# Packing four heads of 32 sample tokens into one tile of 128 rows, in both mixers of a hybrid decoder trunk

## The chip, the cores and the metric

The kernel is one launch on one core of a Trainium2 chip. The metric is the device time of that launch in microseconds (us). The core's engines each work through a queue of their own, in order: TensorE (PE in the profile, PEld for its weight loads), VectorE (DVE), ScalarE (ACT), GpSimd (POOL) and SyncE (SP). They meet at semaphores. TensorE writes only the eight banks of PSUM.

## What is computed

One step of a two-layer decoder for two groups of tokens that share the weights: a prompt of 1024 tokens, and 8 sample sequences of 4 new tokens each (32 tokens) that carry recurrent states. Width 1024, 4 heads.

- Layer 0: a gated DeltaNet mixer (with a spatial gating branch beside it), then a squared-ReLU MLP of width 4096.
- Layer 1: an mLSTM mixer, then the same kind of MLP.

For the sample tokens the gated delta rule comes to this, per sequence `b` and head `h`, on 4 tokens:

```
sol = triangular_solve(I + A, [v * beta, kb * exp(gc)])      # A: masked k k^T, decayed
v_new = u_c - wk_c @ S                  # S: state, 128 x 128
o = qd_c @ S + qk_c @ v_new
S = S * gl_c + kd_c^T @ v_new
```

and the mLSTM to this, with C of 128 x 256 and a vector n of 128 for each `b`, `h`:

```
num = w_inter * (q @ C) + s @ v
den = w_inter * (q @ n) + sum(s)
h = num / max(|den|, exp(-m_t))
C = keep * C + (wk * k)^T @ v
n = keep * n + sum(wk * k)
```

Everything that is not per sequence (scores, decays, solve) is done for all 32 tokens of a head at once under a mask of 4x4 blocks; the products with the states are done for each of the 32 pairs (b, h).

## The kernel before

**Dense work.** The projections and MLPs are a list of units. A unit loads 1024 columns of weights into `wst`, ScalarE rounds them into `whi`, VectorE computes the rest into `wlo` (`lo(u)`, L1665), and TensorE makes three products for each 128x128 block (high·high, low·high, high·low), every record 512 columns wide for prompt tokens 0 to 511 (group 0) or 2 x 272 for the rest with the samples (group 1). A unit is cut into four pieces (`("d", u, p)`); for group 0 a piece is 6 records. `whi` and `wlo` have two buffers. `lo(u + 1)` stands in VectorE's program behind piece 1 of unit u. VectorE also adds the results of the second MLP matrix into the accumulator (L1740) and computes `h1lo` (L1681).

**Mixer work** is spread between those pieces. `Plan.mix` takes the rows of dense pieces and a list `side` of mixer steps, and puts `len(side)/len(rows)` steps behind each row; `("rest",)` is an empty step that only holds a place. All engines run through this one order, so a step's place fixes where it stands on each queue. The samples' delta rule runs in units 102 to 117 (MLP of layer 0, group 0), beside and behind the prompt's tiles 4 to 7; the samples' mLSTM in units 277 to 294 (MLP of layer 1, group 0).

**The samples' steps of the delta rule** (tile `t == TILES`, n = 32): `dec`, `kk`, `kT`, `vT`, `l0`, `la`, `lb`, `zw`, `oT` in `gdn(t, step, q)` do each thing head by head, as four products or transposes of 32 rows. `gdn_sample("vn", j)` makes v_new of heads 2j, 2j+1: for each head one product of the inverse with the right side, then 8 products (one per sequence) of `NWM` (128x32, the columns of the other sequences zeroed) with the state `SS[:, h % 2, b]`, all summed in PSUM. `"o"` does the same with `QDM` for the output. `"u"` makes four state updates at a time: stationary `KM` (32x128), moving `VN` (32x128); VectorE multiplies the old state by its decay and adds (L2052). `SS` holds two heads; POOL stores a head when it is done and loads head h + 2 into its place.

**The samples' steps of the mLSTM**: `mA`, `mB`, `mC`, `mF` in `ml(t, step)`, and in `ml_sample`: `"num"` (per head: 8 products of `QDM` (128x32) with C and n, 257 columns, and one of the scores with v) and `"dc"` (four updates of C: stationary 32x128, moving 32x257; VectorE folds them in, L2209). `CS` holds two heads of C; POOL stores a head (L2636) and loads the head after next (L2591). `rowmask`-products on VectorE (L2039, L2196) zero the keys of the other sequences, 32x512 at a time.

**Records.** A float32 product (`mm`, L605) shows in the trace as two MATMUL records and two LDWEIGHTS records, a transpose as one of each.

Of the kernel before, what the change touches and what calls it, by code (L numbers as in the profile page):

```python
# [5 lines left out]
F32 = mybir.dt.float32  # L6
F32R = mybir.dt.float32r
ALU = mybir.AluOpType
# [25 lines left out]
NL = LEVELS - LB  # L34
FG = 8
# [40 lines left out]
class Plan:  # L76
# [92 lines left out]
    @staticmethod  # L169
    def gdn_sample():  # L170
        t = TILES
        out = [("gx", t), ("gx2", t)] + [("g", t, s, 0) for s in ("act", "gv", "sum", "dec", "kk", "kT", "vT", "l0")]
        out += [("g", t, "la", 1), ("g", t, "lb", 1), ("g", t, "zw", 0), ("gs", "km", 0), ("rest",)]
        for j in range(2):

            out += [("rest",)] * (2 * j) + [("gs", "vn", j), ("gs", "o", j), ("rest",)]
            for h in (2 * j, 2 * j + 1):
                out += [("gs", "u", 2 * h), ("gs", "u", 2 * h + 1), ("rest",)]
            out.append(("rest",))
        out += [("gs", "end", 0), ("rest",), ("rest",), ("rest",), ("g", t, "oT", 0)]  # L180
        return out

    @staticmethod
    def ml(tiles):
        out = []
        for t in tiles:
# [9 lines left out]
            else:  # L196
                out += [("m", t, s) for s in ("mA", "mB", "mC")]
                out.append(("ms", "km", 0, 0))
                for h in range(H):
                    out += [("ms", "num", h, 0), ("ms", "dc", h, 0), ("rest",), ("ms", "dc", h, 1), ("rest",)]  # L200
                out += [("ms", "end", 0, 0), ("rest",), ("rest",), ("m", t, "mF")]
# [129 lines left out]
def build(nc, x_prompt, x_sample, state_gdn, state_gdn_conv, state_mlstm_c, state_mlstm_n, state_mlstm_m,  # L331
# [4 lines left out]
    with ctx:  # L336
# [28 lines left out]
        maskposS = sb("maskposS", [NS, NS])  # L365
        masknegTS = sb("masknegTS", [NS, NS])
# [3 lines left out]
        lmask = sb("lmask", [P, LEVELS, P])  # L370
        lmask0T = sb("lmask0T", [P, P])
        rowmask = sb("rowmask", [NS, NB])
# [62 lines left out]
        def inv_at(t, q, p):  # L435

            return t * (3 + 2 * NL) + (2 * (q - LB) + p + 4 if t < TILES else 2 * q + p + 1)

        def t2_at(t, q, p):

            return t * 2 * NL + 2 * (q - LB if t < TILES else q) + p + 1

        def x_at(t, q, p):

            return t * 2 * NL + 2 * (q - LB if t < TILES else q - 1) + p + 1

        def gdn_map(t):
            n = P if t < TILES else NS
            keys = ["X", "QH", "SQ", "RB", "DT", "QD", "XX", "KB", "KD", "RU", "VB"]
            shapes = [(NCH, n), (8, n), (8, n), (8, n), (H, n), (H, n), (2, 4, n), (H, n)] + [(H, P)] * 3  # L450
            if n == NS:
                keys += ["RW", "NW", "NWM", "QDM", "KM", "SS"]
                shapes += [(H, P), (H, n), (H, NB, NS), (H, NB, NS), (2, 4, P), (2, NB, P)]
# [3 lines left out]
            m["ON"], m["VN"] = m["VB"] if n == P else m["RW"], m["RU"]  # L457
            m["Xi"] = lambda h: m["XX"][0:n, 0, h, :]
# [14 lines left out]
        def ml_map(t):  # L473
# [3 lines left out]
            else:  # L477
                keys = ["X", "WTm", "E", "ST", "KW", "HN", "QDM", "KM", "CS", "NT", "NN", "NROW", "NPR", "BC"]
                shapes = [(NCH, NS)] + [(H, NS)] * 3 + [(H, P), (H, DV + 1), (H, NB, NS), (2, 4, P),
                                                        (2, NB, DV + 1), (NB, H), (NB, H), (P,), (P,), (2, H, NS)]  # L480
# [122 lines left out]
        def _(pe):  # L603
# [186 lines left out]

            def gdn(t, step, q):
                m = gdn_map(t)
                g, c, n = tok(t)
                X, QH = m["X"], m["QH"]
                lv = LEVELS if t < TILES else LEVELS_S
# [33 lines left out]
                elif step == "vT":  # L829
                    w("vsr")  # L830
                    if n == P:
                        w("ke")
                        w("state")
                        for h in range(H):
                            pe.matmul(M4(3)[:, h, :], X[:, 8 + h, :], ident[:, :], is_transpose=True,
                                      start=True, stop=False)
                            last = mm(M4(3)[:, h, :], m["KB"][:, h, :], St[:, h, :], start=False, stop=True)
                    else:
                        for h in range(H):
# [1899 lines left out]
```

## Time and profile before

| | |
|---|---|
| median of 3 runs | 2650.51 us (2650.06 to 2651.29) |
| span of the profiled execution | 2647.3 us |
| TensorE busy | 2584.7 us (98%) |
| VectorE, ScalarE, POOL busy | 1380.3, 1128.1, 244.2 us |
| samples' delta rule | about 815 to 915 us |
| samples' mLSTM | about 1952 to 2087 us |

How to read it: a time such as 845.02 is us from the start of the span; the next number is the duration. A record's duration is its way through a pipeline and overlaps the next one, so what a group of records costs is read from its start to the start of the dense record behind it. `x16` is 16 records merged into one row. `128*32` ahead of the operand's shape is the stationary operand, rows by columns; the last shape is the moving operand.

### The profile page before, as it was taken

The numbers are of one execution on the slowest core, as the hardware profiler recorded it, in microseconds if no ns is written. First come the engines' busy times: TensorE is split into PE (matmuls) and PEld (weight loads), VectorE is DVE, ScalarE is ACT, GpSimd is POOL, SyncE is SP. The second block draws the span as 40 slices with busy tenths as digits, with TensorE's granted clock in tenths as the row PEclk, the third lists the DMA queues.
The fourth block names the chain that finished last, engine by engine and source line by source line (L and its number), as shares of the span: only waits on it lengthen the run. The fifth ranks groups of instructions, "written<-read, shape, count | busy, mean of one in ns | idle before, by whom it ended". The sixth has DMA issues, their size and how long they took to land.

```text
span 2647.3 us, 39319 instructions
## 1 busy us (share of the span) xinstructions
PE 2584.7 (98%) x16324; PEld 2307.5 (87%) x16324; DVE 1380.3 (52%) x2201; ACT 1128.1 (43%) x1914; POOL 244.2 (9%) x396
## 2 busy tenths in 40 slices
PE   8998999999999999999999999999999999999998
PEld 7778888788887798899999989998877888999998
DVE  4746765656564565434444465535544456454344
ACT  6654446455444245333333345433332345333324
POOL 4121111100001001100000001110000000000000
PEclk9999999999999999999999999999999999999999
DMA  6553335533333455533333245554444343333322
GB/s 205 157 156 106 104 113 135 154 101 85 106 95 92 120 144 168 170 120 112 105 95 111 83 131 151 165 150 123 120 120 146 102 121 122 87 111 106 96 88 82
DMA packets 368722, 321.47 MB, mean 121 GB/s; under 512 B 11930, under 2 KB 339668, under 8 KB 368545
## 3 DMA queue, kind: packets, MB, share of 16 engines
q1 hardware_dynamic: 336224, 207.91, 27.2%
q0 software_dynamic: 32320, 111.05, 13.8%
q8 instruction: 130, 2.13, 0.3%
q14 instruction: 48, 0.39, 0.0%
HBM read 261.33 MB, written 57.58 MB: 120 GB/s over the span
## 4 chain that ended last, share of the span: by engine, by line
PE 85%; DVE 6%; ACT 5%; DMA 2%; issue 2%; SPq 0%; POOL 0%; DVEq 0%; ACTq 0%; POOLq 0%
PE dense L605 75%; PE mixer L605 8%; ACT arena L1148 2%; DVE wlo L1665 1%; ACT whi L1148 1%; DMA wst<-in_w_in_even_dram 1%; DVE arena L1890 0%; DVE hf L1806 0%; ACT relu L1148 0%; ACT L1148 0%; DVE hlo L1802 0%; ACT L1153 0%; DMA arena<-xrow 0%; DVE arena L1892 0%; PE mixer L995 0%
## 5 line engine op out<-in xcount | busy, mean ns | idle before, releaser
L605 PE MATMUL dense<-hhi,whi 128*128 128x272 f32 (+1 forms) x3072 | 847.9, 330 | 22.0 <-DVE wlo L1665 15.3
L605 PE MATMUL dense<-hhi,wlo 128*128 128x272 f32 (+1 forms) x3072 | 824.9, 323 | 0.0
L605 PE MATMUL dense<-hlo,whi 128*128 128x272 f32 (+1 forms) x3072 | 824.2, 323 | 0.0
L1665 DVE TENSOR_TENSOR wlo<-wst,whi 128x1024 fp32r<-128x1024 f32 x384 | 471.7, 1228 | 233.2 <-ACT whi L1148 232.3
L605 PEld LDWEIGHTS dense<-hhi,whi 128*128 128x128 f32 x3072 | 515.8, 189 | 78.8 <-DVE wlo L1665 21.1
L1148 ACT ACTIVATE whi<-wst 128x1024 fp32r<-128x1024 f32 x384 | 403.8, 1052 | 423.9 <-PE dense L605 410.5
L605 PEld LDWEIGHTS dense<-hhi,wlo 128*128 128x128 f32 x3072 | 514.1, 189 | 41.7
L605 PEld LDWEIGHTS dense<-hlo,whi 128*128 128x128 f32 x3072 | 516.4, 189 | 37.4 <-issue 0.7
L605 PE MATMUL dense<-h1hi,whi 128*128 128x272 f32 (+1 forms) x1536 | 422.5, 329 | 9.3 <-DVE wlo L1665 5.0
L605 PE MATMUL dense<-h1hi,wlo 128*128 128x272 f32 (+1 forms) x1536 | 414.0, 324 | 0.0
L605 PE MATMUL dense<-h1lo,whi 128*128 128x272 f32 (+1 forms) x1536 | 412.1, 322 | 0.0
L605 PEld LDWEIGHTS dense<-h1hi,whi 128*128 128x128 f32 x1536 | 256.8, 188 | 38.3 <-DVE wlo L1665 8.6
L1681 DVE TENSOR_TENSOR h1lo<-relu,h1hi 128x544 fp32r<-128x544 f32 (+1 forms) x128 | 91.6, 715 | 369.3 <-ACT relu L1148 369.2
L605 PEld LDWEIGHTS dense<-h1hi,wlo 128*128 128x128 f32 x1536 | 257.2, 188 | 21.5
L605 PEld LDWEIGHTS dense<-h1lo,whi 128*128 128x128 f32 x1536 | 257.2, 188 | 21.0 <-issue 0.5
L1148 ACT ACTIVATE relu<-dense 128x512 f32<-128x512 f32 (+2 forms) x132 | 80.6, 611 | 383.8 <-PE dense L605 383.6
L605 PE MATMUL mixer<-arena 128*128 128x128 f32 (+11 forms) x1552 | 231.0, 293 | 11.1 <-DVE arena L1972 8.6
L605 PEld LDWEIGHTS mixer<-arena 128*128 128x128 f32 (+5 forms) x1552 | 193.9, 173 | 50.3 <-issue 21.2
L1740 DVE TENSOR_TENSOR accA<-dense,accA 128x512 f32<-128x512 f32 (+1 forms) x168 | 116.1, 697 | 103.4 <-PE dense L605 103.1
L1756 DVE TENSOR_TENSOR ssum<-ssum,sq 128x512 f32<-128x512 f32 (+1 forms) x98 | 69.2, 707 | 125.7 <-ACT sq L1148 125.6
L1148 ACT ACTIVATE ffh<-dense 128x512 f32<-128x512 f32 (+5 forms) x124 | 62.2, 525 | 167.7 <-PE dense L605 155.7
L1148 ACT ACTIVATE arena<-mixer 128x128 f32<-128x128 f32 (+9 forms) x175 | 63.4, 376 | 101.5 <-PE mixer L605 59.4
(352 smaller groups left out, 1813.6 us busy)
## 6 DMA issues: line engine op xcount, KB each, us to landing
wst<-in_w_ff_dram SPq DMA_DIRECT2D x256, 512.0 KB, 4.0
wst<-in_w_in_even_dram SPq DMA_DIRECT2D x48, 512.0 KB, 4.1
wst<-in_w_in_odd_dram SPq DMA_DIRECT2D x48, 512.0 KB, 4.0
proj<-ffh POOLq DMA_DIRECT2D x48, 272.0 KB, 2.6
proj<-ffh POOLq DMA_DIRECT2D x48, 256.0 KB, 2.3
arena<-proj POOLq DMA_DIRECT2D x16, 512.0 KB, 4.9
wst<-in_w_out_even_dram SPq DMA_DIRECT2D x16, 512.0 KB, 4.1
arena<-proj POOLq DMA_DIRECT2D x8, 1024.0 KB, 8.2
```

Source lines behind the costliest of these rows:

```text
L605: return pe.matmul(out, lhsT, rhs, start=start, stop=stop)
L1148: return act.activation(out, in_, func, **how)
L1665: TT(wlo[:, u % 2, :], wst[:, u % 2, :], whi[:, u % 2, :].bitcast(F32), ALU.subtract)\
L1681: TT(h1lo[:, k, 0:n], r, h1hi[:, k, 0:n].bitcast(F32), ALU.subtract)\
L1740: TT(v, out_of(key, g), v, ALU.add).then_inc(S("dve_evac"), 1)
L1756: ins = TT(ssum[:, 0:n], ssum[:, 0:n], sq2[:, c % 2, 0:n], ALU.add)
```

## The change

Head h's 32 tokens take rows 32h to 32h+31 of one tile of 128 rows.

- Steps that did four heads one after another do one 128x128 product or transpose (`gdn_rows`, `ml_rows`), under masks that are zero between heads. Gates per row come from a product with `spread4` and a masked sum (`own_head`).
- Products with the states stay 32 pairs, but each goes to the band of its head. For v_new, o and num the band is 32 output partitions (the output is `MB[rows_at(h), ...]`); for the updates it is 32 rows of both operands (`KM[rows_at(h), ...]`), and the four heads write four PSUM banks. The loops run over sequences outside and heads inside, so that neighbouring products are in different bands.
- n leaves the 257th column of C: it has a step of its own (`"n"`, two products), and C's products are 256 wide.
- All four heads of the delta rule's state are loaded at once; nothing of it is loaded again. Of C, four sequences (all heads) are in `CS`; sequences 4, 5 and 6, 7 are loaded after 0, 1 and 2, 3 have been stored.
- `vn` and `o` become `vo` (v_new and the state's part of o) and a short `o`; the updates `u` come in two steps of 16 behind `oT`. `num` has two steps and `dc` four steps of 8 updates. The side list of the delta rule is 11 steps shorter and that of the mLSTM 2, which spreads the remaining steps, those of prompt tiles 4 to 7 too, a little wider over the same dense rows.
- The masks at the start are 128 wide instead of 32, and `lmask` has 5 levels instead of 7.

```diff
@@ Plan
-        out += [("g", t, "la", 1), ("g", t, "lb", 1), ("g", t, "zw", 0), ("gs", "km", 0), ("rest",)]
-        for j in range(2):
-
-            out += [("rest",)] * (2 * j) + [("gs", "vn", j), ("gs", "o", j), ("rest",)]
-            for h in (2 * j, 2 * j + 1):
-                out += [("gs", "u", 2 * h), ("gs", "u", 2 * h + 1), ("rest",)]
-            out.append(("rest",))
-        out += [("gs", "end", 0), ("rest",), ("rest",), ("rest",), ("g", t, "oT", 0)]
+        out += [("g", t, "la", 1), ("g", t, "lb", 1), ("g", t, "zw", 0), ("rest",), ("rest",), ("gs", "vo", 0)]
+        out += [("rest",), ("gs", "o", 0), ("rest",), ("gs", "end", 0), ("rest",), ("g", t, "oT", 0), ("rest",)]
+        out += [("gs", "u", 0), ("rest",), ("rest",), ("rest",), ("gs", "u", 1), ("rest",), ("rest",), ("rest",)]
...
+                out += [("m", t, s) for s in ("mA", "mB", "mC")] + [("ms", "n", 0), ("rest",)]
+                for r in range(2):
+                    out += [("ms", "num", r), ("rest",)]
+                    for half in (2 * r, 2 * r + 1):
+                        out += [("ms", "dc", half), ("rest",), ("rest",)]
+                    out += [("rest",)] * (1 - r)
+                out += [("ms", "end", 0), ("rest",), ("rest",), ("m", t, "mF")]
@@ tensor, delta rule
+                elif step == "la":
+                    w("inv", inv_at(t, q - 1, 0))
+                    s(mm(bank(0), rows_of(m["A"]), m["XiT"]), "t2")
...
+                if step == "vo":
...
+                    mm(MB[:, 1, 0:P], m["XiT"], m["RU"], start=True, stop=False)
+                    for b in range(NB):
+                        for h in range(H):
+                            last = mm(MB[rows_at(h), 1, 0:P], m["NWM"][:, h, b, :], m["SS"][:, h, b, :],
                                       start=False, stop=b == NB - 1)
...
+                    for b in range(NB):
+                        for h in range(H):
+                            mm(MB[rows_at(h), 2, 0:P], m["QDM"][:, h, b, :], m["SS"][:, h, b, :],
+                               start=b == 0, stop=False)
...
                     for k in range(4):
-                        last = mm(M4(3 * q)[:, k, :], m["KM"][0:n, q, k, :], m["VN"][0:n, h, :])
+                        for h in range(H):
+                            last = mm(MB[:, h, k * P:(k + 1) * P], m["KM"][rows_at(h), 4 * r + k, :],
+                                      m["VN"][rows_at(h), :])
@@ tensor, mLSTM
+                    for b in range(4 * r, 4 * r + 4):
+                        pe.wait_ge(S(f"s_in{b // 2 % 2}"), 32 * (r + 2))
+                        for h in range(H):
+                            last = mm(MB[rows_at(h), 0, 0:DV], m["QDM"][:, h, b, :], m["CS"][:, b % 4, h, :],
+                                      start=r == 1 and b == 4, stop=b % 4 == 3)
...
+                    for b in (2 * r, 2 * r + 1):
+                        for h in range(H):
+                            last = mm(MB[:, h, b % 2 * DV:(b % 2 + 1) * DV], m["KM"][rows_at(h), b, :],
+                                      V1[rows_at(h), 0, 0:DV])
@@ gpsimd
+                if name == "dc":
+                    pool.wait_ge(S("ms_upd"), r + 1)
+                    for b in (2 * r, 2 * r + 1):
+                        dma(c_s[0, b].rearrange("h k v -> k h v"), m["CS"][:, b % 4]).then_inc(S(f"s_out{r % 2}"), 16)
+                    if r < 2:
+                        pool.wait_ge(S(f"s_out{r}"), 64)
+                        for b in (2 * r, 2 * r + 1):
+                            cs_load(b + 4)
```

TensorE, the first state products of the delta rule. Before, v_new of heads 0 and 1 (18 products) and, six dense records later, their output:

```order
L605 MATMUL mixer<-arena 32x128 x18
L605 MATMUL dense<-h1hi_49,whi 128x512
L605 MATMUL dense<-h1lo_50,whi 128x512
L605 MATMUL dense<-h1hi_49,wlo 128x512
L605 MATMUL dense<-h1hi_49,whi 128x512
L605 MATMUL dense<-h1lo_50,whi 128x512
L605 MATMUL dense<-h1hi_49,wlo 128x512
L605 MATMUL mixer<-arena 32x128 x18
```

Now, all heads' v_new and state output in a row (the first row is the product with the inverse):

```order
L624 MATMUL dense<-h1hi_49,wlo 128x512
L624 MATMUL mixer<-arena 128x128
L624 MATMUL mixer<-arena 32x128 x64
L624 MATMUL dense<-hhi0,whi 128x512
```

Four groups of 18 have become one of 65 and, one unit further on, a single product.

VectorE, the state updates of the delta rule (`gls` holds the decays, `wlo` is `lo(u)`). Before, the first two groups of four:

```order
L2052 SCALAR_TENSOR_TENSOR arena<-arena,gls,mixer 128x128 x4
L2039 TENSOR_TENSOR arena<-arena,rowmask 32x512
L1665 TENSOR_TENSOR wlo<-wst,whi 128x1024
L1740 TENSOR_TENSOR accA<-dense,accA 128x512
L2052 SCALAR_TENSOR_TENSOR arena<-arena,gls,mixer 128x128 x4
```

Now, the first of the two groups, in unit 115:

```order
L1794 TENSOR_TENSOR h1lo<-relu,h1hi 128x512
L2218 SCALAR_TENSOR_TENSOR arena<-arena,gls,mixer 128x128 x16
L1778 TENSOR_TENSOR wlo<-wst,whi 128x1024
L1794 TENSOR_TENSOR h1lo<-relu,h1hi 128x512
L1778 TENSOR_TENSOR wlo<-wst,whi 128x1024
```

Sixteen updates stand in a row now, directly ahead of `lo(116)`.

POOL, the state C of the mLSTM. Before:

```order
L2636 DMA out_dram<-arena 128x8x256
L2591 DMA arena<-in_state_mlstm_c_dram 128x8x256
L2636 DMA out_dram<-arena 128x8x256
L2591 DMA arena<-in_state_mlstm_c_dram 128x8x256
```

Now:

```order
L2811 DMA out_dram<-arena 128x4x256 x2
L2757 DMA arena<-in_state_mlstm_c_dram 128x4x256 x2
L2811 DMA out_dram<-arena 128x4x256 x2
L2757 DMA arena<-in_state_mlstm_c_dram 128x4x256 x2
```

A store or load of 1 MB has become two of half a megabyte; they are bound to sequences now, not to heads.

## Rows read from the trace of the kernel before

**Rows 1.** The page: span, busy time, share of the chain that ended last.
```profile
span 2647.3 us, 39319 instructions
PE 2584.7 (98%) x16324; PEld 2307.5 (87%) x16324; DVE 1380.3 (52%) x2201; ACT 1128.1 (43%) x1914; POOL 244.2 (9%) x396
PE 85%; DVE 6%; ACT 5%; DMA 2%; issue 2%; SPq 0%; POOL 0%; DVEq 0%; ACTq 0%; POOLq 0%
```
**Rows 2.** TensorE by stretches of the samples' stages; first all, then the mixer's bank alone.
```profile
815.00:915.00 100.00, 99.18 (x555) 77.80 (x554) 45.40 (x98) 34.52 (x71) 6.47 (x7) 1.00 0.35 102
1955.00:2090.00 135.00, 133.87 (x577) 97.40 (x577) 64.21 (x111) 38.22 (x65) 7.54 (x10) 1.00 0.44 134
...
815.00:915.00 100.00, 32.85 (x272) 1.00 0.35 102
1955.00:2090.00 135.00, 35.18 (x154) 1.00 0.44 134
```
**Rows 3.** Timeline of TensorE, delta rule: start, duration, engine, line, operation, shapes, records.
```profile
819.39 0.69 PE L605 MATMUL mixer<-arena 128*32 128x32 f32 x16
820.02 0.50 PE L605 MATMUL dense<-hhi,whi 128*128 128x512 f32 x1
820.35 0.39 PE L605 MATMUL dense<-hlo,whi 128*128 128x512 f32 x1
820.58 0.40 PE L605 MATMUL dense<-hhi,wlo 128*128 128x512 f32 x1
...
827.70 0.23 PE L848 MATMUL mixer<-ident,arena 32*32 32x32 f32 x2 [0.82 <-ACT arena L1148]
...
845.02 4.46 PE L605 MATMUL mixer<-arena 32*32 32x128 f32 x36
849.41 0.50 PE L605 MATMUL dense<-h1hi,whi 128*128 128x512 f32 x1
...
859.47 0.39 PE L605 MATMUL dense<-h1hi,wlo 128*128 128x512 f32 x1
859.79 1.15 PE L605 MATMUL mixer<-arena 32*128 32x128 f32 x8
860.87 0.50 PE L605 MATMUL dense<-h1hi,whi 128*128 128x512 f32 x1
```
**Rows 4.** The same for the weight loads (PEld).
```profile
836.07 1.86 PEld L605 LDWEIGHTS mixer<-arena 32*128 32x128 f32 x16 [0.35 <-issue]
...
845.02 0.13 PEld L605 LDWEIGHTS mixer<-arena 32*32 32x32 f32 x2 [0.36 <-issue]
845.35 1.67 PEld L605 LDWEIGHTS mixer<-arena 128*32 128x32 f32 x16 [0.20 <-issue]
847.22 0.13 PEld L605 LDWEIGHTS mixer<-arena 32*32 32x32 f32 x2 [0.20 <-issue]
```
**Rows 5.** Timeline of TensorE, full 128x128 transpose and product (prompt tile), and mLSTM.
```profile
747.19 0.27 PE L835 MATMUL mixer<-ident,arena 128*128 128x128 f32 x1
747.29 0.39 PE L605 MATMUL mixer<-arena 128*128 128x128 f32 x2
747.52 0.27 PE L835 MATMUL mixer<-ident,arena 128*128 128x128 f32 x1
...
1968.68 4.21 PE L605 MATMUL mixer<-arena 128*32 128x257 f32 x18
1972.83 0.50 PE L605 MATMUL dense<-h1hi,whi 128*128 128x512 f32 x1
...
1977.15 2.00 PE L605 MATMUL mixer<-arena 32*128 32x257 f32 x8
1979.07 0.50 PE L605 MATMUL dense<-hhi,whi 128*128 128x512 f32 x1
```
**Rows 6.** Timeline of VectorE around a group of state updates in each mixer.
```profile
901.51 1.12 DVE L2052 SCALAR_TENSOR_TENSOR arena<-arena,gls,mixer 128x128 f32<-128x128 f32 x4 [7.02 <-PE mixer L605]
902.55 0.67 DVE L2039 TENSOR_TENSOR arena<-arena,rowmask 32x512 f32<-32x512 f32 x1
...
1985.11 1.23 DVE L1665 TENSOR_TENSOR wlo<-wst,whi 128x1024 fp32r<-128x1024 f32 x1 [0.26 <-ACT whi L1148]
1986.85 1.78 DVE L2209 SCALAR_TENSOR_TENSOR arena<-arena,keepb,mixer 128x257 f32<-128x257 f32 x4 [0.52 <-PE mixer L605]
```
**Rows 7.** POOL's timeline and the DMA view (KB, us to landing): one state is exchanged.
```profile
1988.92 0.90 POOL L2636 DMA_DIRECT2D out_dram<-arena  x1 [38.47 <-DVE arena L2209]
1994.27 0.88 POOL L2591 DMA_DIRECT2D arena<-in_state_mlstm_c_dram  x1 [4.44 <-DMA out_dram<-arena]
...
arena<-in_state_mlstm_c_dram POOLq DMA_DIRECT2D x4, 1024.0 KB, 7.7
```

More of the change, by code:

```diff
@@ L34 @@
 NL = LEVELS - LB
+LMASK = {q: i for i, q in enumerate([*range(LEVELS_S), *range(LB, LEVELS)])}
 FG = 8
@@ L791, in gdn @@
             def gdn(t, step, q):
+                if t == TILES and step != "sum":
+                    gdn_rows(step, q)
+                    return
                 m = gdn_map(t)
@@ L1035, in ml_sample @@
[L1035 to L1044 removed]
+                        pe.wait_ge(S("ms_upd"), 2)
@@ L1904, in gdn @@
             def gdn(t, step, q):
+                if t == TILES and step != "sum":
+                    gdn_rows(step, q)
+                    return
                 m = gdn_map(t)
@@ new lines, in ml_sample @@
+                if step == "n":
+                    dve.wait_ge(S("ms_n"), 1)
+                    keep = keepb[:, :, 4:].rearrange("p h b -> p b h")
+                    link(TT(m["NN"], m["NT"], keep, ALU.mult))
+                    part = lambda a: MB[:, 3, a:a + NB * H].rearrange("p (b h) -> p b h", h=H)
+                    TT(m["NN"], m["NN"], part(192), ALU.add)
+                    link(TT(m["NT"], part(128), own[:, :, :], ALU.mult))
+                    dve.tensor_reduce(mcol[:, 3:4], m["NT"].rearrange("p b h -> p (b h)"),
+                                      mybir.AxisListType.X, ALU.add).then_inc(S("ms_nset"), 1)
+                elif step == "num" and r:
+                    dve.wait_ge(S("ms_num"), 2)
+                    TT(m["HN"][:, 0:DV], m["HN"][:, 0:DV], MB[:, 0, 0:DV], ALU.add).then_inc(S("ms_kept"), 1)
+                elif step == "dc":
+                    dve.wait_ge(S("ms_dc"), r + 1)
+                    for b in (2 * r, 2 * r + 1):
+                        for h in range(H):
+                            cs = m["CS"][:, b % 4, h, :]
+                            last = STT(cs, cs, keepb[:, h, 4 + b:5 + b], MB[:, h, b % 2 * DV:(b % 2 + 1) * DV],
+                                       ALU.mult, ALU.add)
+                    last.then_inc(S("ms_upd"), 1)
@@ L2623, in ml_x @@
                         .then_inc(S("m_xin"), 16)
-                    cs_load(0)
-                    cs_load(1)
+                    for b in range(4):
+                        cs_load(b)
             def ml(t, name):
```

661 lines of the change are left out of this document (380 added, 281 removed).

## The prediction

> **What bounds the kernel now.** I read the page first. TensorE is busy 98% of the span, and the chain that ended last lies 85% on it, while VectorE is busy 52% [rows 1]. Then the two stretches in which the samples' steps run: 99.18 of 100 us and 133.87 of 135 us of TensorE are busy, VectorE about half, and the granted clock is 1.00, the 2.4 GHz level [rows 2]. Records on the mixer's bank hold 32.85 and 35.18 us of these stretches [rows 2]. So in both stages TensorE's own queue is what ends last: work taken off it comes off the time, and work of other engines counts only where TensorE waits for it. The only wait of size on the samples' path is 0.82 us before the transposes of `l0` [rows 3].
>
> **Prices on TensorE** (from a group's start to the next dense record, which itself comes every 0.23 us [rows 3]):
>
> - Entering and leaving a group costs 0.19 us more than the records: 859.79 - 859.47 = 0.32 in, 820.35 - 820.02 = 0.33 out, each 0.23 otherwise, so 0.09 + 0.10 [rows 3].
> - State product of v_new or o (stationary 128x32, 128 columns): 16 records in 1.67 us, 0.104 a record, 0.21 a product [rows 4]. With 257 columns: 18 records in 4.15, 0.46 a product [rows 5].
> - Update (stationary 32x128): 128 columns 0.96 us of TensorE's pace for four (1.08 from start to start, 0.12 of it the edge), 0.24 a product; 257 columns 1.92 for four, 0.48 [rows 3, 5].
> - Full product 0.23 (747.52 - 747.29), full transpose 0.10 [rows 5].
> - Change of shape inside a group: 0.33 less two records of 0.104 is 0.12, up to the 0.20 that PEld shows as idle [rows 4].
>
> **The change part by part, if bands do not overlap.**
>
> State products of the delta rule: before, four groups of 4.39 us (849.41 - 845.02) and 0.19 each, 18.3 us [rows 3]. After, 64 products at 0.208 are 13.3, two full ones 0.46, edges 0.38, one change 0.16: 14.3. Gain 4.0, since eight small products and most shape changes go. Updates: 8 x (1.08 + 0.19) = 10.2 before; 32 x 0.24 + 2 x 0.3 = 8.3 after. Gain 1.9.
>
> Packed steps of the delta rule: before, `kk` 0.63 [rows 3], `zw` 1.89 (16 records paced by their weight loads, 1.86) [rows 4], six groups of four small transposes or products at about 0.36 and `l0` with its wait 1.2, some 5.9 us. After, `kk` two products 0.46, `kT`, `vT`, `l0`, `oT` one transpose each 0.4, `la` and `lb` 0.46, `zw` one full product and four of 32x128 weights 1.17, `dec` one product more 0.6: 3.1. Gain 2.8, the wait of 0.82 in it: `l0` now comes a unit behind `kk` with no wait on ScalarE's `ru`. Delta rule together 8.7.
>
> mLSTM: `num` 4 x (4.15 + 0.19) = 17.4; after, 33 products at 0.46 and 0.38 make 15.6: 1.8. `dc` 8 x (1.92 + 0.19) and a wait, 17.4; after, 32 x 0.48 + 4 x 0.19 = 16.2: 1.2 [rows 5]. Transposes of v and h go from 16 to 4 records, the scores from four products to one, two products of n and one of the gates are new: gain about 1.0. Together 4.0.
>
> So 12.7 us without any overlap.
>
> **Overlap between bands.** No row of before shows two products in different bands. The bounds come from neighbouring rows. At one end a band changes nothing and the gain above stands. At the other end all four bands run together and a product costs a quarter. I take the middle, for this reason: a product is two records that write the same rows of PSUM, so the second has to follow the first in its band, and if records start in program order, the next head's first record can only start with this head's second. Then two bands run at a time, and a product costs one record instead of two. Floors: a record with 32x128 weights doesn't go below 0.118 us however few its columns (`zw`: 1.89 us for 16 records with 32 columns, and the weight loads fill it) [rows 4]; one with 128x32 weights went at 0.039 (0.63 us for 16) [rows 3]. Hence:
>
> - v_new and o: 64 x 0.104 = 6.7 us gained.
> - num: 32 x 0.23 = 7.4.
> - dc: 32 x 0.24 = 7.7; half of 0.48 is 0.24, just at the floor of two weight loads, 0.236.
> - u: 0.24 is at the floor already, gain 0.
>
> Together 21.8.
>
> The Trainium skill (TensorE: Matmul & The Clock Gate, Part 3) gives 3.07 times the speed for four row bands and 2.38 for three column bands at 512 columns; as an estimate from it, the 51 us of banded products would shrink by some 32 us where I take 21.8. No row of before can show it. Its page TensorEngine Tiling (Key Properties) says that changing the tiling mode drains the array and changing only the tile does not; the 0.12 to 0.20 us above are shape changes, so they agree with the first half, and the second half is what is open here.
>
> **What is late next.** Two waits on TensorE are new.
>
> (1) The exchange of C. Before, from the last update (1986.85 + 1.78) to the landing of the reload (1994.27 + 7.7) took 13.3 us [rows 6, 7]; nobody waited, since the next use of that head lay two heads further on. Now stores and loads are two each, so about 15.1 us (two more issues of 0.9). `dc` 1 stands behind piece 2 of unit 284, `num` 1 behind piece 0 of unit 287: ten pieces of six records, 13.8 us. Counted from the start of `dc` 1 with overlap: TensorE 2.1, VectorE 8 x 0.445 = 3.6 [rows 6], exchange 15.1: landed at 20.9. TensorE asks for sequences 6 and 7 at 2.1 + 13.8 + 0.2 + 1.9 = 18.0. It waits 2.9 us, and in-order dense work waits behind it. Without overlap the same sum gives 22.7 against 21.6, 1.1 us.
>
> (2) Sixteen updates ahead of `lo(116)`. They take 16 x 0.26 = 4.2 us (902.55 - 901.51 is four) and `wlo` 1.23 more [rows 6], so it is ready 5.6 us after `u` 0 ends on TensorE. TensorE has three pieces of unit 115, 4.1 us, and two records, 0.5, before it needs it: wait 1.0. The second group stands behind piece 3 of its unit, and `lo` comes out level; 0.2. The four groups of eight (3.6 us) stand behind piece 2, with `lo` of their unit done already: 0.
>
> Costed at nothing: the key masks on VectorE (8 x 0.67 us per mixer become one pass of about 1.2, hidden under dense work at half load), the wider masks on POOL at the start and three reductions on VectorE there (POOL is busy 9%), the state loads of 2 MB some 40 us ahead of `vo`, the prompt's steps moved by up to four units (same distances or longer; I allow 2 us either way). If the cover of the key masks went, they would cost 1.2 us each.
>
> Sum: 12.7 + 21.8 - 2.9 - 1.2 = 30.4 us less. 2650.5 - 30.4 = 2620.1. The span of 2647.3 lies 3.2 below the median, and I take that as constant.
>
> **The rivals.**
>
> A. Bands don't overlap: 12.7 - 1.1 - 1.2 = 10.4 less, 2640. For it: no row shows an overlap, and records of one shape in the same place queue strictly at their column time. Against it: the bands share neither rows nor banks (updates) or neither columns nor output rows.
>
> B. All four bands run together, weight loads too: the banded 51.1 us (13.3 + 14.7 + 15.4 + 7.7) shrink to 12.8, the reload wait grows to about 4: 12.7 + 38.3 - 5 = 46 less, 2604. Against it: the floor of 0.118 us for 32x128 weights [rows 4] and the shared band of a product's two records. This is where the skill's speed-ups would lead, its estimate above ending near 2610.
>
> C. Slower: every change of band costs what a change of shape costs. There are 64 + 32 + 32 + 32 = 160 such products, each in another band than the one before. At 0.12 to 0.20 us that is 19 to 32 us, and the time 9 to 22 us above the median, 2666 at the 0.16 in between. It decides from 10.4 / 160 = 0.065 us per change. For it: rows 4 show the cost wherever the array is addressed in another way. Against it: in those rows the size of the stationary operand changed as well, here it stays.
>
> D. The bands overlap on one side only (columns, or rows): 30.4 less 7.7, or less 14.1; 2628 to 2634.
>
> **How the numbers follow.** Forecast (two at a time) 0.48, A 0.20, B 0.10, C 0.10, D 0.12. The likeliest gives 2620.1. The range leaves out C and most of B: 2610 to 2643, which takes in A with the allowance of 2 us. A measurement of this kernel can tell about 0.2%, 5.3 us. All but C, and the part of A in which the two waits are larger than I count, come out faster by more: faster 0.85, same 0.05, slower 0.10.
>
> **What would show it.** In the profile of the changed kernel: 64 products of `vo` in about 7 us (forecast), 13.3 (A), 3.5 (B), over 20 (C). Sixteen products of `num` in 3.7 us or 7.4. Eight updates of `dc` in 1.9 us or 3.8. `u` at 3.9 us for sixteen; well below that, the floor of the weight loads is wrong for bands. A wait of TensorE for the load of C of 1 to 3 us near the second `num`, and one of about 1 us for `wlo` behind the first `u`. TensorE's busy time on the mixer's bank falls from 68 us to about 34. The forecast is wrong if the trace shows other rates, or if the waits on TensorE in the delta rule's tiles 4 to 7 grow by more than 2 us.

## The result, and the profile after

The changed kernel took 2609.98 us (median of 4 runs, 2607.28 to 2610.32) against 2650.3 us (2650.06 to 2651.29) on the same chip: a ratio of 0.9843, 95% interval 0.983 to 0.9857. It is 40.3 us faster. The forecast was 30.4 less, 2620, and the range began at 2610: the direction was right, the size was not, and the time lies just under the range.

The page of the changed kernel, its span, engines and the chain that ended last. It answers to [rows 1].

```profile
span 2605.6 us, 39107 instructions
PE 2540.0 (97%) x16251; PEld 2280.9 (88%) x16251; DVE 1372.1 (53%) x2173; ACT 1122.9 (43%) x1885; POOL 251.0 (10%) x406
...
PE 84%; DVE 7%; ACT 5%; DMA 2%; issue 2%; POOL 0%; DVEq 0%; ACTq 0%; POOLq 0%
```

TensorE is still the bound: 44.7 us less busy time, 41.7 us less span. On the mixer's bank its records hold 27.1 us of the two stretches of the samples' steps (813 to 913 and 1952 to 2087 us), where the forecast had about 34 and the kernel before 68. To see where the time went, I cut both traces at the layers' norm sums, which TensorE makes in both kernels. The window view gives, for TensorE in the two stages that hold the samples' steps (delta rule, then mLSTM), the length, busy us, records, granted clock, DMA share and GB/s. Before:

```profile
471.92:944.93 473.01, 464.14 (x2410) 1.00 0.37 105
1676.51:2151.41 474.90, 470.83 (x2573) 1.00 0.44 128
```

After:

```profile
471.11:928.36 457.25, 444.84 (x2358) 0.99 0.38 109
1660.47:2109.46 448.99, 446.33 (x2551) 1.00 0.46 135
```

The delta-rule stage is 15.8 us shorter and the mLSTM stage 25.9, together the whole change; the stretch between them takes 731.6 and 732.1 us. In the first stage TensorE's idle time grew from 8.9 to 12.4 us, in the second it fell from 4.1 to 2.7.

TensorE's timeline after, the groups that the prediction priced, each with the dense record behind it. In order: v_new with the state's part of o (64 banded products and a full one), an update `u` of 16 products, one `dc` of 8 updates, and the second `num`, cut in two by its wait.

```profile
868.66 4.01 PE L624 MATMUL mixer<-arena 128*128 128x128 f32 x130
872.60 0.50 PE L624 MATMUL dense<-hhi,whi 128*128 128x512 f32 x1
...
890.94 1.17 PE L624 MATMUL mixer<-arena 32*128 32x128 f32 x32
892.04 0.50 PE L624 MATMUL dense<-hhi,whi 128*128 128x512 f32 x1
...
1970.48 1.15 PE L624 MATMUL mixer<-arena 32*128 32x256 f32 x16
1971.56 0.50 PE L624 MATMUL dense<-hhi,whi 128*128 128x512 f32 x1
...
1997.95 1.07 PE L624 MATMUL mixer<-arena 128*32 128x256 f32 x16
2000.78 1.07 PE L624 MATMUL mixer<-arena 128*32 128x256 f32 x16 [1.76 <-DMA arena<-in_state_mlstm_c_dram]
2001.78 0.50 PE L624 MATMUL dense<-h1hi,whi 128*128 128x512 f32 x1
```

The group of `vo` takes 872.60 - 868.66 = 3.94 us. At the old price of 0.208 us a product [rows 4] its 64 banded products alone were 13.3. `u` takes 1.10 us for 16 products (3.84 at [rows 3]'s price), `dc` 1.08 for 8 (3.84 by [rows 5]), half a `num` 1.00 for 8 (3.7). With the edges in, these are 3.4 to 3.7 times the speed; the four bands run together, in columns (`vo`, `num`) and in rows (`u`, `dc`) alike. The weight loads of the same groups:

```profile
868.43 3.97 PEld L624 LDWEIGHTS mixer<-arena 128*128 128x128 f32 x130
...
890.94 0.98 PEld L624 LDWEIGHTS mixer<-arena 32*128 32x128 f32 x32 [0.35 <-issue]
```

Thirty-two loads of 32x128 weights fit into 0.98 us, 0.031 each, where the 16 of [rows 4] went at 0.118. That floor held inside one band only. The Trainium skill (TensorE: Matmul & The Clock Gate, Part 3) gives 3.07 times the speed for four row bands and 2.38 for three column bands, at 512 columns; the direction agrees, and here, at 128 and 256 columns, four bands gave more on either side. The Trainium skill (TensorEngine Tiling, Key Properties) says that a change of tile alone does not drain the array; the trace agrees, since 0.06 us a product, the change of band in it, is less than the 0.12 to 0.20 of a change of shape alone [rows 4].

What TensorE waited for in the two stages, by the view of waits (us in total, times, longest). Delta rule, after:

```profile
PE dense L624 <- DVE wlo L1778: 5.1, 5, 1.9
PE dense L624 <- DVE hlo L1915: 4.6, 3, 3.1
PE mixer L624 <- DVE arena L2161: 2.2, 1, 2.2
```

Delta rule, before, where the wait for `wlo` was small:

```profile
PE dense L605 <- DVE hlo L1802: 5.9, 6, 3.1
PE mixer L605 <- ACT arena L1148: 1.1, 1, 1.1
...
PE dense L605 <- DVE wlo L1665: 0.4, 1, 0.4
```

The mLSTM stage, after, the reload of C first:

```profile
PE mixer L624 <- DMA arena<-in_state_mlstm_c_dram: 1.8, 1, 1.8
PE dense L624 <- DVE wlo L1778: 0.5, 1, 0.5
```

and before, 3.3 us of `wlo` that are gone since the prompt's steps moved:

```profile
PE dense L605 <- DVE wlo L1665: 3.3, 4, 1.3
```

The wait for `arena L2161` stands at prompt tile 7 and was in nobody's sum; nor was the longest of those for `wlo`, 1.93 us at 609.7. In e3, with the prompt's steps at their old places, the stage has neither. The wait at tile 7 has a tail, which the timeline shows: dense records behind it start 0.43 us apart instead of 0.23, and the window of 720 to 725 us has a granted clock of 0.66 (1.00 before and behind it), so part of it ran at the 1.2 GHz level.

```profile
719.60 1.35 PE L624 MATMUL mixer<-arena 128*128 128x128 f32 x8 [2.16 <-DVE arena L2161]
720.61 0.78 PE L624 MATMUL dense<-hhi,whi 128*128 128x512 f32 x1
721.18 0.63 PE L624 MATMUL dense<-hlo,whi 128*128 128x512 f32 x1
721.61 0.63 PE L624 MATMUL dense<-hhi,wlo 128*128 128x512 f32 x1
...
720.00:725.00 5.00, 5.00 (x20) 0.66 0.36 109
```

### The profile page after: what moved, and what is told of

Its sections match the earlier page's. It is cut to its first block, busy times and chain, and to the rows that moved or that the text cites. A ratio compares the mean times of both kernels' runs of the same rounds, so it can differ in the third digit from the quotient of the medians.

```text
span 2605.6 us, 39107 instructions
## 1 busy us (share of the span) xinstructions
PE 2540.0 (97%) x16251; PEld 2280.9 (88%) x16251; DVE 1372.1 (53%) x2173; ACT 1122.9 (43%) x1885; POOL 251.0 (10%) x406
## 4 chain that ended last, share of the span: by engine, by line
PE 84%; DVE 7%; ACT 5%; DMA 2%; issue 2%; POOL 0%; DVEq 0%; ACTq 0%; POOLq 0%
PE dense L624 75%; PE mixer L624 6%; ACT arena L1251 1%; DVE wlo L1778 1%; ACT whi L1251 1%; DVE arena L2008 1%; DMA arena<-xrow 0%; DVE arena L2010 0%; DVE hf L1919 0%; PE mixer L690 0%; ACT L1251 0%; ACT relu L1251 0%; DVE hlo L1915 0%; ACT L1256 0%; DMA wst<-in_w_in_even_dram 0%
## 5 line engine op out<-in xcount | busy, mean ns | idle before, releaser
L624 PE MATMUL mixer<-arena 128*128 128x128 f32 (+9 forms) x1500 | 186.8, 296 | 14.0 <-DVE arena L2154 8.6
L624 PEld LDWEIGHTS mixer<-arena 128*128 128x128 f32 (+4 forms) x1500 | 164.9, 176 | 36.8 <-DVE arena L2154 9.9
L1251 ACT ACTIVATE arena<-mixer 128x128 f32<-128x128 f32 (+7 forms) x167 | 60.6, 377 | 96.6 <-PE mixer L624 48.0
```

The source lines that it names most:

```text
L624: return pe.matmul(out, lhsT, rhs, start=start, stop=stop)
L1251: return act.activation(out, in_, func, **how)
```

## The experiments

Two things had to be told apart: why four bands run at once although the prediction allowed two, and where the delta rule lost what it gained. All times are medians of 4 runs; before took 2650.4 to 2651.1 beside them.

### The order of the products

**e0, the changed kernel itself**, as the neighbour of the others.

> The changed kernel once more, as the neighbour of the next three. Both theories: 2607 to 2611 us; 64 banded products of v_new and o in 3.7 us of the mixer's group of 3.94; TensorE waits near the second num for the load of C (1 to 3 us).

Measured: 2609.7 us, ratio 0.9848 (0.9833 to 0.9862). The reload of C was late by 2.89 us in this execution, by 1.76 in the first one.

**e1, heads outside, sequences inside**: runs of 8 products (16 records) in one band for `vo`, 4 products (8 records) for `u` and `num`, 2 products (4 records) for `dc`.

```diff
+            def turns(bs):
...
+                return [(b, h) for h in range(H) for b in bs]
...
-                    for b in range(NB):
-                        for h in range(H):
...
+                    for b, h in turns(range(NB)):
```

> Only the order of the banded products changes: heads outside, sequences inside, so 8 (v_new, o), 4 (num, u) and 2 (dc) products in a row go to one band; num waits for both halves of C first. Theory 'neighbours': bands overlap only where neighbouring records are in different bands, so the v_new and o group goes from 3.9 us to about 13, num from 2.4 to about 7, u from 1.1 to about 3.5, and the time to about 2635 (2628 to 2642). Theory 'own queues': each band works through its own records and TensorE looks far enough ahead to feed them; the groups stay within 20% and the time at 2608 to 2614.

Measured: 2627.75 us, ratio 0.9913 (0.9898 to 0.9927). `vo`, `u` and one `dc` in its timeline:

```profile
870.53 11.62 PE L624 MATMUL mixer<-arena 128*128 128x128 f32 x130
882.08 0.50 PE L624 MATMUL dense<-hhi,whi 128*128 128x512 f32 x1
...
900.43 2.82 PE L624 MATMUL mixer<-arena 32*128 32x128 f32 x32
903.17 0.50 PE L624 MATMUL dense<-hhi,whi 128*128 128x512 f32 x1
...
1985.56 1.17 PE L624 MATMUL mixer<-arena 32*128 32x256 f32 x16
1986.65 0.50 PE L624 MATMUL dense<-hhi,whi 128*128 128x512 f32 x1
```

The same products in the same bands cost 18 us more, and the groups themselves account for 16.6 of it, so the order carries that much of the 40 us. (The edit also makes `num` wait for both halves of C, 3.10 us against 2.89 in e0.) But it does not act as all or nothing, and the time lies between the two expectations: `vo` at 11.55 us is below the serial sum of 13.3 and 0.6, `u` at 2.74 below its 3.84, and `dc`, in runs of four records, takes 1.09 against 1.08 in e0.

**e2, two bands at a time**: heads 0 and 1 alternate over all sequences, then 2 and 3.

```diff
...
+                return [(b, h) for p in ((0, 1), (2, 3)) for b in bs for h in p]
```

> Order in pairs: all sequences of heads 0 and 1 in turn, then of heads 2 and 3, so two bands take turns. Theory 'neighbours': twice the cost of four bands: 0.104 us a product, v_new and o group about 7, num about 4, u about 2; time about 2620 (2616 to 2625). Theory 'own queues': between that and no change, less than 5 us slower. If the prediction's reason were right (two bands at a time at most), this would change nothing in any group.

Measured: 2615.57 us, ratio 0.987 (0.9855 to 0.9884).

```profile
868.72 6.29 PE L624 MATMUL mixer<-arena 128*128 128x128 f32 x130
874.95 0.50 PE L624 MATMUL dense<-hhi,whi 128*128 128x512 f32 x1
```

6.23 us for `vo`, and a time just under the 2616 to 2625 expected. This is what the prediction's rule (two bands at a time) would look like, and the changed kernel does not look like it.

**e4, runs of two products**: four records of a band in a row, then the next band.

```diff
...
+                return [(b, h) for i in range(0, len(bs), 2) for h in range(H) for b in bs[i:i + 2]]
```

> The changed kernel with the same products in another order: in v_new, o, u and num two products of one head (four records) stand in a row before the next head's, instead of one (two records); dc already goes two products a head in the changed kernel's pair of sequences and is written the same way here. Theory H (a band holds about four records that run or wait, and the queue behind them stands only when a fifth comes): runs of four records still leave all four bands filled, so the group of 64 products of vo stays at 3.9 to 4.6 us, u at 1.1 to 1.5, num at 2.4 to 2.9 for its first part, the time 2608 to 2613. Theory N (only neighbouring records overlap, a record starts when the one ahead has started and its own band is free): every second neighbour is in the same band, so the banded products take about half the serial time or more: vo 7 us or more, u about 2, num about 4, and the time is 2609.7 + 3.3 + 1.8 + 3.4 = 2618. The runs of 16, 8 and 4 records of the kernel with heads outside overlapped 1.2, 1.4 and (dc) fully; H is what would tie these together.

Measured: 2610.94 us, ratio 0.9847 (0.9832 to 0.9862).

```profile
869.94 4.08 PE L624 MATMUL mixer<-arena 128*128 128x128 f32 x130
873.95 0.50 PE L624 MATMUL dense<-hhi,whi 128*128 128x512 f32 x1
...
892.29 1.29 PE L624 MATMUL mixer<-arena 32*128 32x128 f32 x32
893.50 0.50 PE L624 MATMUL dense<-hhi,whi 128*128 128x512 f32 x1
```

4.01 us for `vo` and 1.21 for `u`: theory H as expected. That only neighbouring records overlap (7 us) is out. One sentence of the expectation is not so: in the changed kernel `dc` has one product of a head in a row, not two, so this edit changes it too; it takes 1.10 us here.

**e9, `vo` in runs of four products** (eight records), everything else as in the changed kernel.

```diff
...
+                return [(b, h) for i in range(0, len(bs), 4) for h in range(H) for b in bs[i:i + 4]]
```

> The changed kernel with v_new and o in runs of four products (eight records) a head; u, num and dc as in the changed kernel. A quantitative form of theory H, drawn from the kernel with heads outside: the next band starts when three records of the present one are still outstanding, so a run of R records costs R - 3 of them, and the last run R. Sixteen runs of eight: 15 x 5 + 8 = 83 records of 0.104 us = 8.6, and 0.4 to 0.5 for the full products and the edges: the group of vo takes 9.0 to 9.2 us instead of 3.95, and the time is 2609.7 + 5.1 = 2614.8. Rival W (a window over the whole queue of about 16 records, whatever their bands): at eight records a run two bands run at a time, 6.9 to 7.2 us, 2612.8. Rival O (the loss is paid once for each change of band, however long the runs, at the size that 11.5 us with 7 changes shows): more changes would cost more, so more than 11.5 us.

Measured: 2615.28 us, ratio 0.987 (0.9854 to 0.9886).

```profile
867.61 8.37 PE L624 MATMUL mixer<-arena 128*128 128x128 f32 x130
875.91 0.50 PE L624 MATMUL dense<-hhi,whi 128*128 128x512 f32 x1
```

The time is 5.6 above e0, near the 5.1 expected; the group itself takes 8.30 us. A window over the whole queue (W, 7.2 at most) is too fast, a fixed loss per change of band (O, above 11.5) too slow; H is nearest, but with 9.0 it was 0.7 too high. The look-ahead w of a band, in records, can be worked out anew. In e0, `vo` has all bands full: 128 records x 0.104 / 4 = 3.3 us, so 0.6 of its 3.94 are the two records of the full product and the edges. Then e9's 7.7 us are 74 records in line; with 16 runs of 8, 15 x (8 - w) + 8 = 74 gives w = 3.6. e1's `vo`, 10.9 us or 105 records, gives 7 x (16 - w) + 16 = 105, w = 3.3. Its `u` gives 3.3 in the same way, and its first `num` (5.05 us, with records of 0.23) 4.1. The e2 group follows without a free number: two bands make half of 13.3, 6.7, less three changes of pair at some 3.5 x 0.104, and 0.6: 6.2, measured 6.23.

The trace also holds the start of every single record (the timeline merges neighbours into one row), and these starts show the same without a fit. In e1's `vo` the records of a band start 0.109 us apart, and the first record of the next band starts at 872.180, 0.006 us behind the thirteenth of sixteen: three of the band's records are still waiting then, and they start behind it. In e9's `vo` the next band starts behind the fifth of eight records, and so it does in e1's `u` and in its first `num`, where records are 0.216 us apart. Three are waiting each time. So w is one number; the spread from 3.3 to 4.1 comes of the rounded price (0.104 for 0.109) and of some 0.03 us that each new band loses. The expectation of e9 had the three right and the cost wrong by one: a run of R records costs R - 4 of them and 0.03 us, 0.467 us for eight.

So one rule holds for all these groups: a band takes four records, one that runs and three that wait, and a fifth makes the queue stand; up to there the records of the next band go in beside them. No window over the whole queue fits, whatever its size: one of four or five records would explain e1 and e9, but in e4 four bands start within 0.04 us (870.247 to 870.287), the last with twelve records ahead of its first one in the queue. The Trainium skill (TensorE: Matmul & The Clock Gate, Part 3) speaks of a 64-deep reorder window for weight loads. If a window of that depth alone decided, the runs of eight records would have overlapped by more than their last three; they did not, and the measurement decides.

### The delta rule's waits

**e3, the prompt's steps at their old places**: 11 and 2 empty steps put back into the two side lists.

```diff
+        out += [("rest",)] * 11
...
-                out += [("ms", "end", 0), ("rest",), ("rest",), ("m", t, "mF")]
+                out += [("ms", "end", 0), ("rest",), ("rest",), ("m", t, "mF"), ("rest",), ("rest",)]
```

> The changed kernel with 11 and 2 empty steps behind the samples' steps, so that the prompt's steps of tiles 4 to 7 stand behind the same dense rows as before the change. Theory 'places': the new waits and the lower clock of the delta rule's stage (7.7 us of waits against 3.0 before, clock 0.79 against 0.91 at 480 to 500 us) come from the wider spread; they go, and the stage between the norm at 471 us and the norm at 928 us is 4 to 8 us shorter: 2602 to 2606. Theory 'bursts': they come from the samples' own steps and from chance, and the time stays within 2 us of the changed kernel.

Measured: 2604.96 us (2603.45 to 2609.05), ratio 0.9831 (0.9815 to 0.9848). Its stages:

```profile
471.08:925.42 454.34, 443.80 (x2359) 0.99 0.39 110
1657.54:2107.28 449.74, 444.87 (x2551) 1.00 0.46 135
```

The delta-rule stage is 454.3 us instead of 457.3 (first execution) and 458.6 (e0): the wait of 2.16 us at tile 7 and its slow clock are gone (1.00 in 720 to 725), and so is the 1.93 at 610, behind which e0 had a slow stretch too. One part of the expectation failed: the low clock at 480 to 500 us stayed (0.83), and e0, with the wide spread, has 0.93 there, so the spread is not its cause. Such stretches between 475 and 490 us took 1.7 to 5.1 us of clock from one execution to the next, whatever the kernel (1.7 in e0, 3.4 in e3, e6 and e7, 5.1 in the first execution and in e8), and each stage length here is of one execution. The mLSTM stage is as before the edit, within its spread (449.0, 450.8). The interval of the time still meets that of the changed kernel, so the stages say it more surely than the medians. What is left in the first stage are two waits for `wlo`, 1.17 us behind the first `u`, and 2.36 behind the stores of the state: TensorE's record and, ahead of it, ScalarE's, which waited for the weights themselves.

```profile
895.50 0.50 PE L625 MATMUL dense<-h1hi,whi 128*128 128x512 f32 x1 [2.36 <-DVE wlo L1779]
```

```profile
893.13 1.06 ACT L1252 ACTIVATE whi<-wst 128x1024 fp32r<-128x1024 f32 x1 [3.41 <-DMA wst<-in_w_ff_dram]
```

**e6, `u` in four steps of 8** (from e3), stores still all behind the last.

```diff
-        out += [("gs", "u", 0), ("rest",), ("rest",), ("rest",), ("gs", "u", 1), ("rest",), ("rest",), ("rest",)]
-        out += [("rest",)] * 11
+        for j in range(4):
+            out += [("gs", "u", j), ("rest",), ("rest",)]
+        out += [("rest",)] * 7
...
-                    for k in range(4):
+                    for k in (2 * (r % 2), 2 * (r % 2) + 1):
...
```

> e3 with the delta rule's update u in four steps of 8 products and 8 VectorE updates instead of two of 16; stores of the states all at the end, as before. My theory (16 updates in a row, 4.2 us, hold up the quantisation wlo of the next unit, which TensorE asks for): bursts of 8 take 2.1 us and the wait for wlo behind u 0 (1.17 us in e3) goes; the two new entries and exits of a small group cost 2 x 0.19 + 2 x about 0.3 (less overlap at each group's ends) = 0.7 to 1.0 us; time within 0.5 us of e3. Rival (wlo is late there because the weights or the activations are late, not VectorE): the wait stays and the time is 1 us more. In both the wait of 2.36 us for wlo behind the stores of the state stays.

Measured: 2602.59 us (2600.9 to 2603.25), ratio 0.9816 (0.9802 to 0.9831). The delta-rule stage takes 451.3 us, 3.1 less than e3, where I expected no gain. TensorE's waits for `wlo` there fell from 3.9 to 1.7 us: the one of 1.17 is gone, as expected, and the one of 2.36, which was to stay, is 1.33. Its busy time fell by 1.1 although the smaller groups cost about 0.8 more, as priced (0.66 us for 8 products, 1.10 for 16, and two more entries): e3's granted clock of 0.91 at 891 to 911 us, around the wait of 2.36, is 1.00 here. What I had missed in the sum was that a wait can have a slow stretch behind it.

**e7, the new state stored in four pairs** (from e6), each pair of sequences behind its own `u`.

```diff
-                if name == "u" and r == 3:
-                    pool.wait_ge(S("gs_new"), 4)
-                    for h in range(H):
-                        dma(gdn_s[0, :, h].rearrange("b k v -> k b v"), gdn_map(TILES)["SS"][:, h])\
+                if name == "u":
+                    pool.wait_ge(S("gs_new"), r + 1)
+                    for b in (2 * r, 2 * r + 1):
+                        dma(gdn_s[0, b].rearrange("h k v -> k h v"), gdn_map(TILES)["SS"][:, :, b])\
...
```

> The previous kernel (u in four steps) with the new delta-rule state stored in four pairs of 256 KB, one pair behind each u, instead of 2 MB in four transfers at once behind the last. Theory (the 2 MB of stores issued together delay the next unit's weights; ScalarE waited 3.41 us for wst at 893.1 in e3, and TensorE 2.36 us for wlo that follows from it): the wait for DMA shrinks below 1 us and the 2.36 us go, time 1.5 to 2.5 us under e3, 2602.5 to 2603.5. Rival (the weights are late there for another reason, such as the loads of xl or the state of the mLSTM that are issued near by): the wait stays at 2 to 3.5 us and the time is within 0.5 us of e6's.

Measured: 2602.6 us (2600.64 to 2604.3), level with e6. The mechanism came out as expected: ScalarE's wait for `wst`, 3.05 us in e6, is gone, `wlo` costs TensorE 0.4 us in the stage, and the stage takes 449.6, 1.7 less. The time stayed because the other stage became 1.5 longer. There both kernels wait 1.9 us for the reload of C, and only e7 got a slow clock behind it. e6, then e7:

```profile
1990.00:1995.00 5.00, 5.00 (x28) 3.82 (x21) 2.43 (x4) 0.00 (x0) 0.00 (x0) 1.00 0.34 95
```

```profile
1990.00:1995.00 5.00, 5.00 (x22) 3.78 (x15) 2.25 (x3) 0.00 (x0) 0.00 (x0) 0.66 0.32 94
```

Six records fewer in 5 us, at 0.66. Why one execution falls and the other doesn't, with waits of 1.94 and 1.93 us, no row shows; it stays open.

**e5, the second `num` two steps later** (from e3).

```diff
-                    out += [("rest",)] * (1 - r)
-                out += [("ms", "end", 0), ("rest",), ("rest",), ("m", t, "mF"), ("rest",), ("rest",)]
+                    out += [("rest",)] * 3 * (1 - r)
+                out += [("ms", "end", 0), ("rest",), ("rest",), ("m", t, "mF")]
```

> The kernel with the two mixers' steps at their old places (e3), and in the mLSTM two of its empty steps moved to between the second dc and the second num, which so stands 15 instead of 13 steps behind. Nothing is computed otherwise. My theory (the exchange of C takes about 20 us from the start of the second dc, and TensorE asks for the last two sequences 2 to 3 us too early): the wait for DMA in the second num (1.95 us in e3) goes, nothing else changes, and the time is 2.0 us less, 2603. Rival (the load lands later whenever it is asked for later, since the queue it stands in is held by the weights' loads, or another wait follows it): the wait moves or another takes its place, time within 0.5 us of e3's 2605.0.

Measured: 2603.52 us (2602.47 to 2605.19), ratio 0.9823 (0.9806 to 0.9839). The wait is gone from the list and the mLSTM stage takes 447.60 us instead of 449.74, the 2.1 expected. The medians differ by 1.4 and their runs overlap; the stage is what shows it.

**e8, all three edits together.**

> The three edits of places together: u in four steps, each pair of sequences of the new delta-rule state stored behind its own step, and the second num of the mLSTM 15 steps behind the second dc. Theory (each edit removes its own wait, and they don't touch each other): taken from the stages that each edit changed, u in four steps gave 3.1 us (454.3 to 451.3 between the norm sums of the delta-rule stage), the spread stores 1.7 more (451.3 to 449.6), the later num 2.1 (449.7 to 447.6 in the mLSTM stage); in all 6.9 under e3, 2598.1. Rival (a wait removed in one place comes back behind it, as in the kernel with spread stores, whose time stayed at 2602.6 because its mLSTM stage took 451.25 instead of 449.74 at a granted clock of 0.94 in 30 us behind the reload wait): the time is 2600.5 to 2603.

Measured: 2600.21 us (2598.51 to 2600.69), ratio 0.9808 (0.9793 to 0.9822).

```profile
472.29:922.00 449.71, 442.98 (x2359) 0.99 0.39 111
1654.14:2101.79 447.65, 444.74 (x2552) 1.00 0.46 136
```

Both stages came out as their single edits had them (449.6, 447.6), so the edits add up and no wait came back. The time of 2600.2 lies 2.1 above the sum I had made, and just under the rival's 2600.5 to 2603, so the medians alone would not decide: the sum was made from stages against e3's median, whose runs spread over 5.6 us. In the profiled executions the two stages gave 6.7 us and the time 5.5; the other 1.2 were lost ahead of the delta-rule stage, which begins at 472.3 us in e8 and at 471.1 in e3, with the same work before it. e8 beats the changed kernel by 9.8 us and the kernel before by 50.2.

## Why the prediction was off

**The gain without overlap (12.7).** No run shows the large groups packed and serial, since even e1 overlaps, so 8.7 and 4.0 can't be read as such. What can be read are the small packed steps, edges in and waits out: 6.5 us before and 4.2 after in the delta rule, 2.3 less where 2.0 was forecast (2.8 less its wait, which is gone too); 3.2 and 2.1 in the mLSTM, 1.1 for a forecast of 1.0.

**The overlap (21.8): the step that failed.** The prediction reasoned that a product's second record must follow its first in its band, and that records start in program order, so two bands run at a time. The first half stands. The second was an assumption, and the trace refutes it: in the changed kernel's `vo` four records start within 0.02 us (868.968 to 868.988), the next four from 869.101 on, and records of one band are 0.109 us apart, so the first records of three other heads start ahead of a head's second. e4 shows that even four records in a row in one band leave all four bands busy. The queue does not stand at the first record whose band is taken; it stands at the fifth. From there the terms follow, each with its edges as in the forecast:

- `vo` and `o`: forecast 14.3 - 6.7 = 7.6 us; measured 3.94 and 0.11, and 0.22 for `o`, 4.3 in all, 3.3 better. (`vo` costs nothing to enter: its first product is a full one and starts 0.23 us behind the dense record.)
- `u`: 8.3; measured 2 x 1.10 and edges, 2.6: 5.7 better. Here the floor of 0.118 us for a weight load failed too, which I had read in one band and applied to four. It was the largest single miss, and a value of zero that no row proved.
- `num`: 8.2; measured 2.39 and 2.07 (its wait out), with edges 4.8: 3.4 better.
- `dc`: 8.5; measured 4 x 1.08 and edges, 5.1: 3.4 better.

Together 16 us more than forecast. Rival B (all bands together) had the right mechanism, 2604 and a chance of 0.10. I held two correct rows against it, and both were from a single band.

**The waits.** The reload of C was forecast at 2.9 us and took 1.76 to 3.10 in the executions that kept its place: right. `wlo` behind the first `u`: 1.0 (by its own terms 0.8, since 4.2 and 1.23 are 5.4 and not 5.6), measured 1.31. Behind the second: 0.2, measured 0.64. "Two microseconds either way" for the moved steps of the prompt was too small and hid two real effects of opposite sign. From 490 to 815 us, where the prompt's tiles 4 to 7 run, TensorE waited 0.69, 0.39 and 1.08 us before and 1.93 and 2.16 after, 1.9 more, which is just short of the 2 us that the prediction named as a sign against it; the rates of the groups were the other sign, and that one came.

**Why the total missed by 10 and not by 16.** In the delta-rule stage the forecast was 14.2 less and 15.8 came. From group start to next dense record, waits taken out, all mixer groups of the stage sum to 86.8 us before (79 groups) and 65.4 after (71), and the edges of the samples' groups to 3.8 and 1.5: 23.7 us of TensorE's work. Of it 3.5 went into idle time and 5.1 into the clock. The last is read from the windows of 5 us in which the granted clock is below 1: one minus the clock, times 5, sums to 1.7 us before and, with the window at 720 us above, to 6.8 after. In these rows it is the third number from the end. Before:

```profile
480.00:485.00 5.00, 3.48 (x8) 2.06 (x9) 4.93 (x7) 1.26 (x2) 0.15 (x1) 0.66 0.09 27
```

After:

```profile
475.00:480.00 5.00, 1.18 (x6) 0.52 (x5) 3.68 (x5) 3.93 (x6) 1.83 (x2) 0.81 0.90 257
480.00:485.00 5.00, 4.25 (x9) 2.46 (x9) 4.96 (x7) 1.74 (x3) 0.00 (x0) 0.50 0.22 61
485.00:490.00 5.00, 5.00 (x15) 3.43 (x15) 3.50 (x6) 1.53 (x4) 0.00 (x0) 0.67 0.15 45
```

That leaves 15.1, 0.7 less than measured. The extra 9.0 of overlap were thus largely eaten by waits and slow clock that my sum didn't have, and that the total came within 10 us is luck. e3, e6 and e7 gave 7.6 us back (457.25 to 449.61), of which 1.7 is the stretch at 475 to 490 us, which no edit aimed at.

In the mLSTM stage the forecast was 16.2 and 25.9 came: 6.8 more from `num` and `dc`, 2.8 from waits for `wlo` that vanished with the moved steps (3.3 to 0.5; 2.6 again in e3, where they stand at their old places), 1.1 since the reload was late by 1.8 and not by 2.9, and 1.7 lost again in a slow stretch at 1725 to 1735 us (granted clock 0.74 and 0.92), whose cause no row shows. That makes 25.2.

**The rivals.** A and C are refuted: bands overlap, and 160 changes of band cost nothing visible (0.06 us a product, all told). D too: rows and columns both overlap.

## What to carry to other kernels

When small products are packed into bands of the array, put neighbours in different bands, with at most four records (two float32 products) of a band in a row; the same instructions in runs of eight products cost three times as much (11.5 against 3.9 us). Where a row shows a floor or an order constraint, ask whether it was seen in one band or across bands before it is carried over. Then look at what the shorter queue now waits for: here moved steps of the prompt, bursts on VectorE, 2 MB of stores beside weight loads and a reload asked for too early were worth another 10 us.

## What was not expected of the hardware

- Weight loads overlap across bands as the products do: 0.031 us for each of 32 loads of 32x128, against 0.118 in one band.
- A band takes four records, one running and three waiting, before the queue stands, for records of 128 and of 256 columns alike (e1, e9), and the next band's first record then starts ahead of those three.
- A wait of TensorE of about 2 us can be followed by a stretch at the lower clock (0.66 over 5 us, 1.7 us lost), and need not be. It came in e7 and not in e6 behind the same wait; behind the 2.16 us at tile 7 it came in four of six executions (not in e1 and e2), behind the 1.93 at 610 us in three of the same six (e0, e1, e2).
